# Panel products in three passes, rotated copies by shuffles and half copies

## What is computed

```
for l in range(2):
    proj = rms_norm(h, attn_norm[l]) @ w_in[l]                 # 1024 x 7424
    dq, dk, dv, rq, rk, rv, rg, gq, gk, gv, gate = split(proj)
    dq, dk = partial_rope(rms_norm(dq)), partial_rope(rms_norm(dk))   # 16 of 64 columns turned
    rq, rk = rope(rq), rope(rk)                                # 128 columns, halves of 64
    gq, gk = axial_rope(rms_norm(gq)), axial_rope(rms_norm(gk))       # two groups of 32
    a = differential_attention(dq, dk, dv); c = grouped_query_attention(gq, gk, gv)
    r = bidirectional_retention(rq, rk, rv)
    h = h + (sum of sigmoid(gate) * (branch @ w_branch)) @ w_out[l]
    h = h + square(relu(rms_norm(h, mlp_norm[l]) @ w_mlp_in[l])) @ w_mlp_out[l]

def apply_rope(x, cos, sin):                                   # x1, x2: the halves of x
    return concat([x1 * cos - x2 * sin, x2 * cos + x1 * sin])
```

## Time and profile before

| | us |
|---|---|
| median of 3 runs | 1932.89 |
| lowest, highest | 1930.7, 1933.24 |
| the profiled execution, its own time | 1930.86 |
| its span, first to last instruction | 1929.1 |
| TensorE busy | 1869.6 (97%) |
| VectorE busy | 1269.8 (66%) |
| GpSimd busy | 590.2 (31%) |
| ScalarE busy | 356.8 (18%) |

### The profile page before, as it was taken

How to read it: one execution, slowest core, us unless ns; L and a number is a source line. 1 busy time by engine, 2 the same in 40 slices (tenths; PEclk the granted TensorE clock), 3 DMA queues, 4 the chain that set the end, 5 groups by cost and what they waited for, 6 DMA issues and landing times.

```text
span 1929.1 us, 32922 instructions
## 1 busy us (share of the span) xinstructions
PE 1869.6 (97%) x13570; PEld 1712.2 (89%) x13570; DVE 1269.8 (66%) x1424; ACT 356.8 (18%) x655; POOL 590.2 (31%) x745
## 2 busy tenths in 40 slices
PE   4999999998999999999999999999999999999999
PEld 2777777887989979999999998999999999999999
DVE  6663222436268987666687976876667897687666
ACT  3100000103121221211132123321112212432110
POOL 1111111111236313333333222343434332244333
PEclk8999999999999999999999999999999999999999
DMA  9335665331333425354544333444554433344452
GB/s 367 118 109 217 252 245 216 129 109 44 110 132 117 157 88 181 148 179 177 193 154 153 134 131 129 153 175 176 188 181 175 153 132 131 120 162 172 180 180 104
DMA packets 44912, 307.35 MB, mean 159 GB/s; under 512 B 5376, under 2 KB 5888, under 8 KB 8320
## 3 DMA queue, kind: packets, MB, share of 16 engines
q1 hardware_dynamic: 40912, 292.66, 41.4%
q10 hardware_dynamic: 3888, 13.03, 1.9%
HBM read 302.53 MB, written 3.15 MB: 158 GB/s over the span
## 4 chain that ended last, share of the span: by engine, by line
PE 88%; DVE 7%; DMA 1%; issue 1%; ACT 1%; POOL 1%; SPq 0%; DVEq 0%; ACTq 0%; POOLq 0%
PE ps L1898 26%; PE ps L1899 25%; PE ps L1900 25%; PE ps L2030 2%; DMA landing<-in_stream 1%; DVE wlo L681 1%; DVE wlo L683 1%; PE ps L2397 1%; DVE xlo L745 1%; PE ps L2421 1%; PE ps L2407 1%; PE ps L2246 1%; PE ps L2291 1%; PE ps L2370 1%; PE ps L2299 1%
## 5 line engine op out<-in xcount | busy, mean ns | idle before, releaser
L1898 PE MATMUL ps<-xhi,whi 128*128 128x256 f32 (+1 forms) x3680 | 1116.1, 303 | 13.1 <-DVE xlo L691 3.0
L1899 PE MATMUL ps<-xlo,whi 128*128 128x256 f32 (+1 forms) x3680 | 1099.3, 299 | 0.0
L1900 PE MATMUL ps<-xhi,wlo 128*128 128x256 f32 (+1 forms) x3680 | 1098.9, 299 | 0.0
L1898 PEld LDWEIGHTS ps<-xhi,whi 128*128 128x128 f32 x3680 | 705.4, 192 | 50.0 <-issue 18.0
L1899 PEld LDWEIGHTS ps<-xlo,whi 128*128 128x128 f32 x3680 | 705.6, 192 | 22.2 <-issue 1.2
L1900 PEld LDWEIGHTS ps<-xhi,wlo 128*128 128x128 f32 x3680 | 705.2, 192 | 21.0
L681 DVE TENSOR_TENSOR wlo<-landing,whi 128x1024 fp32r<-128x1024 f32 x242 | 428.4, 1770 | 256.5 <-POOL whi L617 255.8
L615 POOL TENSOR_TENSOR whi<-landing,ones 128x16 fp32r<-128x16 f32 x242 | 67.1, 277 | 1321.2 <-PE ps L1900 1281.7
L683 DVE TENSOR_TENSOR wlo<-landing,whi 128x1024 fp32r<-128x1024 f32 x242 | 295.3, 1220 | 0.0
L618 POOL TENSOR_SCALAR whi<-landing 128x1024 fp32r<-128x1024 f32 x242 | 265.0, 1095 | 0.0
L617 POOL TENSOR_SCALAR whi<-landing 128x1008 fp32r<-128x1008 f32 x242 | 261.4, 1080 | 0.1
(11 more groups left out here) (265 smaller groups left out, 1256.7 us busy)
## 6 DMA issues: line engine op xcount, KB each, us to landing
landing<-in_stream SPq DMA_DIRECT2D x250, 1024.0 KB, 4.8
ws<-in_stream SPq DMA_DIRECT2D x28, 1024.0 KB, 5.2
spectra<-big ACTq DMA_DIRECT2D x8, 256.0 KB, 4.3
ws<-spectra ACTq DMA_DIRECT2D x2, 1024.0 KB, 5.1
ws<-in_tabs ACTq DMA_DIRECT2D x1, 1280.0 KB, 5.4
h<-in_xT ACTq DMA_DIRECT2D x1, 1024.0 KB, 6.3
ws<-in_ctxT ACTq DMA_DIRECT2D x1, 1024.0 KB, 15.3
ws<-in_window ACTq DMA_DIRECT2D x1, 1024.0 KB, 13.3
```

What stands on the lines that cost most here:

```text
L1898: mm(out, w_hi, x_hi, start=first, stop=False, skip_group_check=True)
L1899: mm(out, w_hi, x_lo, start=False, stop=False, skip_group_check=True)
L1900: return mm(out, w_lo, x_hi, start=False, stop=last, skip_group_check=True)
```

## The change

Four things are changed.

- A panel's products go in three passes over all its chunks and accumulators: high weights with high activations, high weights with low activations, low weights with high activations. TensorE waits for the high part of a panel (`hi_done`) at its start and for the low part (`lo_done`) before the third pass; row panels wait for `act_hi` first and for `act_lo` before the second. The last panel of a row stage keeps the old order by banks. `streamed` takes the chunks two by two, each pass two chunks behind the one before, and begins on high parts of activations; `last_panel` does the three passes for each half of the chunks. Sums that stood in the middle of a panel now stand ahead of its third pass.
- A new count `hi_used` goes up after a panel's second pass. GpSimd's `high` waits for it, and for the low part of the panel two back, instead of for `panel_used`. VectorE's `low` waits as before.
- The rotated copies aren't made by TensorE. For the first four groups VectorE's `stream_shuffle` exchanges rows within each 32 partitions, from SBUF to SBUF; for RQ and RK ScalarE copies the upper 64 partitions to the lower and the other way round (`head_swap`, after step 14's turn and after the first exponentials). The sign is in the sine tables, which the host lays out.
- The ropes move: RQ from step 15 to 14, RK from 17 to 16, GK from 14 to 18, GK's scaling from 13 to 15. In the steps from 16 on the rope stands behind the softmax weights. `scores(0)` also waits for the last head norm on ScalarE; scores and retention wait for the ropes in the new order.

The core of the diff (for the new passes only the added lines; callers are changed to fit):

```diff
@@ -101,6 +101,8 @@
+SWAP8 = [i ^ 8 if i < 16 else i for i in range(32)]
+SWAP16 = [i ^ 16 for i in range(32)]
+        for h, sign in ((0, -1), (8, 1)):
+            tabs["sin_part"][b + h:b + h + 8] = sign * np.sin(a).T
...
+        ROPES = ((DQ, 4, "dq_norm", SWAP8, "cos_part", "sin_part"), (DK, 4, "dk_norm", SWAP8, "cos_part", "sin_part"),
+                 (GQ, 4, "gq_norm", SWAP16, "cos_axial", "sin_axial"), (GK, 2, "gk_norm", SWAP16, "cos_axial", "sin_axial"),
+                 (RQ, 4, None, None, "cos_ret", "sin_ret"), (RK, 4, None, None, "cos_ret", "sin_ret"))
-        ROT_AFTER = {8: (0, 0), 10: (1, 0), 12: (2, 0), 13: (3, 0), 14: (4, 14), 16: (5, 16)}
-        SCALE_IN = {8: 0, 10: 1, 12: 2, 13: 3}
-        ROPE_IN = {9: 0, 11: 1, 13: 2, 14: 3, 15: 4, 17: 5}
+        SCALE_IN = {8: 0, 10: 1, 12: 2, 15: 3}
+        ROPE_IN = {9: 0, 11: 1, 13: 2, 14: 4, 16: 5, 18: 3}
+        ROPE_ORDER = (0, 1, 2, 4, 5, 3)
@@ -609,7 +611,8 @@
             def high(g, s, turn, n=PANEL):
                 pool.wait_ge(landed[s], (turn + 1) * 16)
                 if not isinstance(g, int) or g >= N_LEAD + 2:
-                    pool.wait_ge(panel_used, g - 1)
+                    pool.wait_ge(hi_used, g - (N_LEAD + 1))
+                    pool.wait_ge(lo_done, g - (N_LEAD + 1))
                 hi, panel = whi[:, s % 2], landing[:, s]
 
                 pool.tensor_tensor(hi[:, 0:FIRST], panel[:, 0:FIRST], ones[:, 0:FIRST], ALU.mult)
@@ -1172,15 +1175,21 @@
                                            ALU.mult, ALU.mult).then_inc(rp_n, 1)
 
                 def head_rope(n):
-                    c, w, _, _, cs_, sn = ROPES[n]
-                    x = chunks(c, w)
-                    dve.wait_ge(rp_rot, at(rp_rot, l, n + 1))
+                    c, w, gain, swap, cs_, sn = ROPES[n]
+                    x, turned = chunks(c, w), nrot[:, 4 - w:4]
+                    if gain:
+                        dve.wait_ge(rp_n, at(rp_n, l, n + 1))
+                    else:
+                        dve.wait_ge(rp_swap, at(rp_swap, l, n - 3))
+                    if ROPE_ORDER.index(n):
+                        dve.wait_ge(rp_done, at(rp_done, l, ROPE_ORDER.index(n)))
                     def wide(name):
                         return tb(name).unsqueeze(1).to_broadcast([P, w, T])
-                    v.tensor_tensor(nrot[:, 0:w], ps[:, 4:6].rearrange("p b (c t) -> p (b c) t", t=T)[:, 0:w], wide(sn),
-                                    ALU.mult)
+                    if swap:
+                        lstep(v.stream_shuffle(turned, x, swap))
+                    v.tensor_tensor(turned, turned, wide(sn), ALU.mult)
                     lstep(v.tensor_tensor(x, x, wide(cs_), ALU.mult))
-                    v.tensor_tensor(flatc(c, w), flatc(c, w), nrot[:, 0:w].rearrange("p c t -> p (c t)"), ALU.add
+                    v.tensor_tensor(flatc(c, w), flatc(c, w), turned.rearrange("p c t -> p (c t)"), ALU.add
                                     ).then_inc(rp_done, 1)
                 def evict(i):
                     dve.wait_ge(panel_used, l * PER_LAYER + (G_LAYER + i + 1))
@@ -1313,11 +1322,11 @@
                     if n in RET_OUT:
                         decayed(RET_OUT.index(n))
                     low_next(i)
-                    if i in ROPE_IN:
-                        head_rope(ROPE_IN[i])
                     if n == 12:
                         centre()
                     weights(n)
+                    if i in ROPE_IN:
+                        head_rope(ROPE_IN[i])
                     if n == 11:
                         subln_scale()
                     if n + 1 in RET_SCORES[1:]:
@@ -1772,9 +1781,18 @@
                         act.wait_ge(rp_n, at(rp_n, l, n))
                     rms(nrs[:, 0:w], ps[:, 2:4].rearrange("p b (c t) -> p (b c) t", t=T)[:, 0:w], 64, 0, lstep
                         ).then_inc(rp_rs, 1)
+                def head_swap(n):
+                    c, w = ROPES[n][:2]
+                    act.wait_ge(proj_out, at(proj_out, l, (14, 16)[n - 4] - N_VALUES))
+                    act.wait_ge(rp_done, at(rp_done, l, n - 1))
+                    a.activation(nrot[0:64, 0:w], chunks(c, w)[64:128], ACT.Identity)
+                    a.activation(nrot[64:128, 0:w], chunks(c, w)[0:64], ACT.Identity).then_inc(rp_swap, 1)
+
                 for i in range(N_HEADS):
                     if i < N_VALUES:
                         projected(i)
+                    if i == 14:
+                        head_swap(4)
                     if i == 0:
                         lam_parts()
                     if i in RMS_AFTER:
@@ -1825,6 +1843,8 @@
                 for n in range(PAIRS):
                     expo(n)
+                    if n == 0:
+                        head_swap(5)
                     if n in RET_SCORES:
                         g = RET_SCORES.index(n)
                         act.wait_ge(rt_arg, at(rt_arg, l, g + 1))
@@ -1893,56 +1913,95 @@
...
+            def highs_in(g):
+                pe.wait_ge(hi_done, 2 * g - 2 * (N_LEAD - 1))
+
+            def lows_in(g):
+                pe.wait_ge(lo_done, g - (N_LEAD - 1))
+
+            def one_pass(w, x, s, job, first=False, last=False, ks=range(KD)):
+                outs, x0, n, token = job
+                for k in ks:
+                    for c, (out, opens) in enumerate(outs):
+                        if token:
+                            a, b = x[:, k, x0 + c * P:x0 + (c + 1) * P], w[:, s % 2, k * COLS:k * COLS + n]
+                        else:
+                            a, b = w[:, s % 2, k * COLS + c * P:k * COLS + (c + 1) * P], x[:, k, x0:x0 + n]
+                        ins = mm(out, a, b, start=first and opens and k == ks[0], stop=last and k == ks[-1],
+                                 skip_group_check=True)
+                return ins
+
+            def panel(g, s, *jobs, beside=None):
+                highs_in(g)
+                for job in jobs:
+                    one_pass(whi, xhi, s, job, first=True)
+                for job in jobs:
+                    last = one_pass(whi, xlo, s, job)
+                last.then_inc(hi_used, 1)
+                if beside is not None:
+                    beside()
+                lows_in(g)
+                for job in jobs:
+                    last = one_pass(wlo, xhi, s, job, last=True)
+            def feature(outs, x0, t):
+                return outs, x0, t, False
+
+            def token(outs, x0, n):
+                return outs, x0, n, True
+
+            def row_panel(g, s, row, r, outs, t, first, last):
+                def one(w, x, opens_all, ends):
+                    for k in range(ROWK):
+                        for j, (out, opens) in enumerate(outs):
+                            c = slice(k * D + j * P, k * D + (j + 1) * P)
+                            ins = mm(out, w[:, s % 2, c], x[:, r % 2, k, 0:t], start=opens_all and opens and k == 0,
+                                     stop=ends and k == ROWK - 1, skip_group_check=True)
+                    return ins
+                highs_in(g)
+                pe.wait_ge(act_hi, row + 1)
+                one(whi, ahi, first, False)
+                pe.wait_ge(act_lo, row + 1)
+                one(whi, alo, False, False).then_inc(hi_used, 1)
+                lows_in(g)
+                return one(wlo, ahi, False, last)
+
+            def row_panel_by_banks(g, s, row, r, outs, t, first, beside=None, order=range(KD)):
+                highs_in(g)
+                lows_in(g)
+                pe.wait_ge(act_lo, row + 1)
+                        hi, lo, a, b = whi[:, s % 2, w], wlo[:, s % 2, w], ahi[:, r % 2, k, 0:t], alo[:, r % 2, k, 0:t]
+                        mm(out, hi, a, start=first and opens and k == 0, stop=False, skip_group_check=True)
+                        ins = mm(out, hi, b, start=False, stop=False, skip_group_check=True)
+                        if n == KD - 1 and k == ROWK - 1:
+                            ins.then_inc(hi_used, 1)
+                        ins = mm(out, lo, a, start=False, stop=k == ROWK - 1, skip_group_check=True)
+                    if n % 2 and n < KD - 1:
+            def streamed(g, s, job, base, order=range(KD), per=1, ends=True):
+                highs_in(g)
+                for n in range(0, KD + 4, 2):
+                    if 4 <= n:
+                        if n == 4:
+                            lows_in(g)
+                        last = one_pass(wlo, xhi, s, job, ks=order[n - 4:n - 2], last=n == KD + 2)
+                    if 2 <= n < KD + 2:
+                        pe.wait_ge(norm_lo, base + per * n)
+                        ins = one_pass(whi, xlo, s, job, ks=order[n - 2:n])
+                        if n == KD and ends:
+                            ins.then_inc(hi_used, 1)
+                    if n < KD:
+                        pe.wait_ge(norm_hi, base + per * (n + 2))
+                        one_pass(whi, xhi, s, job, ks=order[n:n + 2], first=n == 0)
@@ -1951,19 +2010,20 @@
...
```

(22 more changed lines are left out.)

155 lines of the change are left out of this document (43 added, 112 removed).

## The result

| | before | after |
|---|---|---|
| median of 4 runs, us | 1932.31 | 1920.97 |
| lowest, highest | 1930.7, 1933.24 | 1920.65, 1921.28 |
| the profiled execution, its span | 1930.86, 1929.1 | 1920.65, 1918.8 |
| ratio to before, 95% interval | | 0.9945 (0.9932 to 0.9958) |

The change makes the kernel faster, by 11.3 us. 34.8 us were forecast (1898, range 1889 to 1915): the sign is right, the size is a third, and the time lies outside the range.

What follows compares the result with a forecast made beforehand. TensorE was taken as the bound, busy 1869.6 of 1929.1 us. Terms 19.8 + 1.0 + 14.0 = 34.8 us off 1930.86 gave 1896.1, stated as 1898 because the median lies 2.0 us higher; range 1889 to 1915.

Steps and rivals of the forecast that it cites:

- Rotations leave TensorE: 88 matmul records between panels go, 18.9 us, with a 0.9 us wait on a scaled head: 19.8 us saved.
- What takes their place: Shuffles add 4.3 us of VectorE a layer, ScalarE half copies 2.1 us a rope; nothing booked against the saving.
- I take covered: From 1019 to 1097 us VectorE's 71.3 us falls to 64.7 without collisions, so the added work costs TensorE nothing.
- the third rival: VectorE becomes the bound, ropes' first multiplies collide with GpSimd, low parts keep colliding: 16.2 us saved, 1917; chance 0.04.
- Softmax weights: Weights go ahead of ropes in VectorE's queue; half of the 2.1 us wait goes: 1.0 us, bounds 0 and 2.1.
- Panels in three passes: Panel products keep steps of 0.12 us; waits on low parts, folded sums and streamed panels go: 14.0 us saved.
- Rival 4: 324 added waits inside panels stop TensorE's instruction supply, 0.19 us each, 61.6 us: slower, 1960; chance 0.06.
- L681 and the folds behind it start earlier: At the first boundary GpSimd's earlier high part brings the folds forward, so the sums' 1.9 us wait on L762 goes.
- the 0.88 us at each streamed panel: Behind four boundaries high products run ahead, 8 matmuls remain after the last low part; 3.5 us in all.
- rival 1: Only the rotations' 19.8 us come; each boundary wait that goes returns on the next VectorE result: 1913; chance 0.13.
- Rivals 2 and 3: 2: VectorE bounds from 1019 to 1097 us, costing 8.6 us, 1907, chance 0.10. 3: the third rival, 1917, chance 0.04.

Runs made afterwards that it cites:

- e2: Kernel before with the panel half of the change alone (three passes, `hi_used`, new wait of `high`), rotations still by matmuls: 1926.05 us, ratio 0.9971.
- e12: Changed kernel with GpSimd's high part again waiting for the whole of the panel two back, as before the change: 1917.16 us, ratio 0.9934.
- e9: Changed kernel with ScalarE instead of GpSimd making the high parts of projection panels 8 to 23 of each layer: 1917.66 us, ratio 0.9927.

## Why the prediction was right or wrong

**Rotations leave TensorE (19.8 us): right as a term.** The records are gone, and from i = 3 to 15 the first layer is 8.25 us shorter.

**What takes their place: wrong, and this is the step that failed.** The shuffles were priced right (1.32 us against 1.21; 4.7 us a layer against 4.3), and so were ScalarE's half copies (1.06 us each). What failed is "I take covered". The prediction had 71.3 us of VectorE's work against 67 of TensorE's and argued that collisions would go: 8 x 0.83 = 6.6 us. e2 shows that they do go in the new panel order when the ropes are as before. With the new ropes they come back elsewhere: GpSimd doesn't work less, so on a VectorE that is never idle its passes meet whatever stands there, the ropes, L686, L1265. There the earlier start, for which 6.6 us of relief were booked, relieved VectorE of nothing: 81.09 us busy with it (after), 80.43 without (e12). e9 prices what was left out: 10.2 us a layer. The relief was counted and the same passes landing on other instructions weren't. The second ground for "covered", a lag of some 5 us that costs nothing, was read off the evictions. On those TensorE waits 0.5 us in after; the lag ends at the softmax weights, and there it costs 10.7 us of waits.

The rule of the Trainium skill (SBUF — State Buffer, section Who interferes with whom) had been set against the change as the third rival. L1190 at 1.95 and 2.08 us agrees with it, and e9 shows its cost. The prediction's "the trace agrees in both rows" says too much: L681 in the earlier trace rows does, but GpSimd had ended at 1058.69 us, before L1180 began at 1060.82, so that row shows nothing of what happens beside GpSimd. (The stretch also has ten low parts, not eleven; eight of them are the long ones.) That rival put the extra work at 10 us in both layers and gave 1917, with a chance of 0.04; it erred in sparing all but the ropes' first multiplies and L681.

**Softmax weights (1.0 us): wrong.** Their waits grew from 2.1 to 10.7 us. The ropes behind the weights delay the next step's weights, which the prediction said and priced at half of 2.1.

**Panels in three passes (14.0 us): the step of 0.12 us right, the waits mostly wrong; 5.9 us came (e2).** Rival 4 falls: 124 panels of after take 5.76 us from start to start, 48 steps of 0.12 us, so the waits inside them cost nothing. The waits on L683 went. The six on L691 became two of 1.3 us, and two of 0.96 us are new at the first branch panels. The profile names no cause for these; in the first layer the panel starts 0.1 us behind an eviction (L1197 at 1190.24, 0.69 us; TensorE at 1191.03). Both kinds come with GpSimd's earlier start (e12). The wait on L762 stayed, at 2.2 us: the folds are done 3.7 us earlier (981.89 against 985.60), but TensorE is there 4.0 us earlier too (979.50 against 983.48, the last panel matmul ahead of the sums). All of the boundary is that much earlier, its first addition by 4.1 us (958.82 against 962.91) and its first fold by 4.3 (974.76 against 979.02), so "L681 and the folds behind it start earlier" did not come: GpSimd's earlier start gave the folds 0.2 us, and then ran beside them (in after L763 took 1.51 us at 975.38 and 0.68 at 979.31). From 982.6 to 986.0 us the granted clock was 0.50 behind that wait, and some 13 matmuls took 0.213 instead of 0.120 us, 1.2 us more. Of the 0.88 us at each streamed panel little can have come: the waits on VectorE's low parts of the stream are 2.9 us where L745's were 1.3, the case of rival 1.

**The rivals and the range.** Rivals 2 and 3 were the true ones, with 0.14 together, and rival 1 held for the streamed panels. They aren't exclusive: each takes its part from the same sum. The range took each by itself and ended at 1915; all three together lie beyond it.

## What to carry to other kernels

Work moved from the bounding engine onto one that is 67 of 78 us busy isn't covered by a share below one: add it up in the stretch where it lands and ask who waits within that stretch. Where two engines hold each other up, price the helper's passes on whichever instruction they will meet after the change; a collision that leaves one instruction lands on the next one if that engine has no idle time. Starting a helper earlier is worth something only where somebody waits for it. Before work is handed to a third engine, look at that engine's own queue: here ScalarE came late in its turn.
